# Grouped heads in two attention stages of a two-block transformer kernel on one core

## The reference, cut to what matters

```
def sliding_window_attention_with_sinks(q, k, v, sinks):   # 12 query heads, 4 key heads, 64 wide
    ...                                                    # each query block of 128 sees its own and the previous block
    scores = jnp.where(mask[None, :, None, None], scores, NEG_INF)
    m = jnp.maximum(jnp.max(scores, axis=-1, keepdims=True), sink)
    e = jnp.exp(scores - m)
    probs = e / (jnp.sum(e, axis=-1, keepdims=True) + jnp.exp(sink - m))
    out = jnp.einsum("bnkgqc,bnckd->bnqkgd", probs.astype(v.dtype), vb)

def memory_attention(q, mk, mv):                           # 4 heads, 64 wide, 256 memory tokens
    s = jnp.einsum("bshd,bmhd->bhsm", q, mk).astype(jnp.float32) * (HEAD_DIM ** -0.5)
    p = jax.nn.softmax(s, axis=-1).astype(mv.dtype)
    o = jnp.einsum("bhsm,bmhd->bshd", p, mv)
```

## Time and profile before

| what | value |
|---|---|
| median of 3 runs | 2321.39 us (2320.91 to 2326.01) |
| profiled execution, its own time | 2317.27 us |
| span of the profiled execution | 2315.3 us |
| TensorE busy | 2062.4 us, 89% |
| VectorE busy | 1187.1 us, 51% |
| ScalarE busy | 1000.4 us, 43% |
| mean granted TensorE clock | 0.914 |

### The profile page before, as it was taken

The page is one execution under the profiler, slowest core; times in us unless marked ns, Lnnn a source line. Parts: engine busy times, 40 slices in busy tenths (PEclk is TensorE's granted clock), DMA queues, the critical chain, the costliest instruction groups (busy, mean ns, idle before and its releaser), DMA issues.

```text
span 2315.3 us, 41908 instructions
## 1 busy us (share of the span) xinstructions
PE 2062.4 (89%) x16886; PEld 1777.1 (77%) x16886; DVE 1187.1 (51%) x1933; ACT 1000.4 (43%) x1636; POOL 139.1 (6%) x122
## 2 busy tenths in 40 slices
PE   5998999889999999998788899987789997788998
PEld 4883787777877877887778799976579986357997
DVE  5321787725433433545455376455466556546654
ACT  5332577324322323544322265447255554325543
POOL 0000000001000001002332000100010000001000
PEclk8999999869999999899999799999699999559999
DMA  8330576502333332322000166643246663004664
GB/s 264 86 114 9 154 222 188 164 8 78 105 91 91 100 91 85 98 78 81 4 3 3 33 174 185 193 118 100 73 128 189 176 180 109 0 1 139 186 174 119
DMA packets 441805, 254.62 MB, mean 110 GB/s; under 512 B 10816, under 2 KB 440512, under 8 KB 441536
## 3 DMA queue, kind: packets, MB, share of 16 engines
q1 hardware_dynamic: 441664, 252.59, 37.6%
HBM read 251.51 MB, written 1.05 MB: 109 GB/s over the span
## 4 chain that ended last, share of the span: by engine, by line
PE 81%; DVE 10%; ACT 6%; issue 2%; DMA 1%; POOL 0%; DVEq 0%; ACTq 0%; SPq 0%; POOLq 0%
PE bank L378 19%; PE bank L380 19%; PE bank L379 19%; PE bank L370 4%; PE bank L941 2%; PE bank L603 2%; PE bank L604 2%; DVE weights_lo L328 2%; PE bank L1876 2%; ACT weights_hi L321 1%; PE bank L947 1%; PE bank L1168 1%; PE bank L1978 1%; PE bank L611 1%; PE bank L1892 1%
## 5 line engine op out<-in xcount | busy, mean ns | idle before, releaser
L328 DVE TENSOR_TENSOR weights_lo<-ring,weights_hi 128x1024 fp32r<-128x1024 f32 x472 | 577.7, 1229 | 472.3 <-ACT weights_hi L321 468.9
L378 PE MATMUL bank<-x_hi,weights_hi 128*128 128x256 f32 (+1 forms) x2024 | 646.7, 320 | 80.9 <-DVE x_lo L406 29.0
L321 ACT ACTIVATE weights_hi<-ring 128x1024 fp32r<-128x1024 f32 x472 | 495.4, 1054 | 348.5 <-PE bank L380 311.6
L380 PE MATMUL bank<-x_hi,weights_lo 128*128 128x256 f32 (+1 forms) x2024 | 640.5, 316 | 0.0
L379 PE MATMUL bank<-x_lo,weights_hi 128*128 128x256 f32 (+1 forms) x2024 | 640.2, 316 | 0.0
L378 PEld LDWEIGHTS bank<-x_hi,weights_hi 128*128 128x128 f32 x2024 | 391.5, 193 | 115.2 <-issue 86.8
L379 PEld LDWEIGHTS bank<-x_lo,weights_hi 128*128 128x128 f32 x2024 | 391.7, 194 | 25.3 <-issue 1.2
L380 PEld LDWEIGHTS bank<-x_hi,weights_lo 128*128 128x128 f32 x2024 | 391.5, 193 | 23.4
L378 PE MATMUL bank<-hidden_hi,weights_hi 128*128 128x256 f32 (+1 forms) x864 | 271.0, 314 | 10.0 <-DVE hidden_lo L1442 6.8
L380 PE MATMUL bank<-hidden_hi,weights_lo 128*128 128x256 f32 (+1 forms) x864 | 269.7, 312 | 0.0
L379 PE MATMUL bank<-hidden_lo,weights_hi 128*128 128x256 f32 (+1 forms) x864 | 268.9, 311 | 0.0
(11 more groups left out here) (312 smaller groups left out, 2500.5 us busy)
## 6 DMA issues: line engine op xcount, KB each, us to landing
ring<-mlp_w SPq DMA_DIRECT2D x128, 512.0 KB, 4.0
ring<-ada_w SPq DMA_DIRECT2D x96, 512.0 KB, 4.7
ring<-w_ffn_in SPq DMA_DIRECT2D x88, 512.0 KB, 4.7
ring<-w_ffn_out SPq DMA_DIRECT2D x32, 512.0 KB, 3.8
ring<-gdn_w_in SPq DMA_DIRECT2D x24, 512.0 KB, 3.9
ring<-even_w_in SPq DMA_DIRECT2D x18, 512.0 KB, 4.7
ring<-w_out SPq DMA_DIRECT2D x16, 512.0 KB, 4.9
ring<-w_in_a SPq DMA_DIRECT2D x14, 512.0 KB, 3.8
```

What stands on the lines that cost most here:

```text
L321: nc.scalar.activation(w_hi[:, g % AHEAD, :], ring[:, g % RAW, :], ACT.Copy).then_inc(hi_done[g % AHEAD].sem, 1)
L328: nc.vector.tensor_tensor(w_lo[:, g % AHEAD, :], ring[:, g % RAW, :], w_hi[:, g % AHEAD, :].bitcast(F32), ALU.subtract).then_inc(lo_done[g ...
L378: pe.matmul(dst, lhs[0](k), rhs[0](k), start=start and k == 0, stop=False)
L380: last = pe.matmul(dst, lhs[1](k), rhs[0](k), start=False, stop=stop and k == nk - 1)
```

## The change

Both attentions are now run by a new class, `Grouped`, over groups of heads. In a memory attention a group is two heads and a block of 128 queries: 4 groups for each attention. In the sliding-window attention there are six groups of two heads for the second query block (256 keys) and four groups of three heads for the first (128 keys). The heads of a group are every second one, so that their outputs have the same half of the partitions and go out in one copy. For a group VectorE has one mask addition, one maximum, one negation, one reciprocal, one multiplication (by a reciprocal that is broadcast along each head's columns) and one copy of the output. ScalarE still has one exponential for each head, and one copy of the transposed probabilities for each group. TensorE has the same matmuls and transposes as before, in another order: scores of group i, transposes of group i-2, product of group i-3. Scores have three PSUM banks, probabilities three rooms.

A sink is a further column of its head's scores, written by GpSimd (scaled by 8, since the exponential scales by 1/8), so that the maximum and the sum take it in by themselves. VectorE waits for GpSimd's column ahead of the maximum.

In layer B the memory groups stand first; they need no rotated queries. The three rotations of the queries are done by VectorE after the maximum of groups 0, 1 and 2. The scores of the sliding-window groups wait for all five rotations, and no longer the first scores.

```
+            def pe(self, pe, ready=None):
+                for i in range(self.n + 3):
+                    if i < self.n:
+                        ...
+                        self.wait(pe, att_max, i - 3)
+                        self.wait(pe, att_exp, i - 3)
+                        for x, hd in enumerate(self.groups[i]["heads"]):
+                            ins = pe.matmul(self.scores(i)[:, x, :], hd["q"], hd["k"], start=True, stop=True)
+                        ins.then_inc(att_scores.sem, 1)
+                    if 0 <= i - 2 < self.n:
+                        j = i - 2
+                        g, (to, _) = self.groups[j], self.turned(j)[0]
+                        self.wait(pe, att_probs, j)
+                        self.wait(pe, att_probsT, j - 2)
+                        for x in range(len(g["heads"])):
+                            for b in range(g["nk"] // P):
+                                at = x * g["nk"] + b * P
+                                ins = pe.transpose(to[:, at:at + P], self.probs(j)[:, x, b * P:(b + 1) * P], ident)
+                        ins.then_inc(att_turned.sem, 1)
+                    if i - 3 >= 0:
+                        j = i - 3
+                        g, (_, pt) = self.groups[j], self.turned(j)[0]
+                        self.wait(pe, att_probsT, j)
+                        self.wait(pe, att_out, j - 2)
+                        for x, hd in enumerate(g["heads"]):
+                            ins = product(pe, self.mixed(j)[:, x * P:(x + 1) * P], lambda b: hd["v"][b],
+                                          lambda b: pt[:, x * g["nk"] + b * P:x * g["nk"] + (b + 1) * P], len(hd["v"]))
+                        ins.then_inc(att_mixed.sem, 1)
+
+            def dve(self, dve, between=None):
+                for i in range(self.n + 3):
+                    if i < self.n:
+                        g, src = self.groups[i], self.scores(i)
+                        self.wait(dve, att_scores, i)
+                        self.wait(dve, att_probs, i - 3)
+                        if "mask" in g:
+                            self.wait(dve, att_turned, i - 3)
+                            m = g["mask"].rearrange("p (o k) -> p o k", o=1).broadcast_to((P, len(g["heads"]), g["nk"]))
+                            link(dve, nc.vector.tensor_tensor(self.probs(i), src, m, ALU.add))
+                            dve.wait_ge(att_sinks.sem, self.sunk[i])
+                            src = self.wide(i)
+                        link(dve, nc.vector.reduce_max(self.small(i, 0), src, AX.X))
+                        nc.vector.tensor_scalar(self.small(i, 1), self.small(i, 0), -self.scale, None, ALU.mult)\
+                            .then_inc(att_max.sem, 1)
+                        if between is not None:
+                            between(dve, i)
+                    if 0 <= i - 1 < self.n:
+                        j = i - 1
+                        g = self.groups[j]
+                        self.wait(dve, att_exp, j)
+                        link(dve, nc.vector.reciprocal(self.small(j, 3), self.small(j, 2)))
+                        r = self.small(j, 3).rearrange("p (h o) -> p h o", o=1).broadcast_to((P, len(g["heads"]), g["nk"]))
+                        nc.vector.tensor_tensor(self.probs(j), self.probs(j), r, ALU.mult).then_inc(att_probs.sem, 1)
+                    if i - 3 >= 0:
+                        j = i - 3
+                        self.wait(dve, att_mixed, j)
+                        nc.vector.tensor_copy(self.groups[j]["out"], self.mixed(j).rearrange("p (h t) -> p h t", t=P))\
+                            .then_inc(att_out.sem, 1)
...
+            def pool(self, pool):
+                for i in self.sunk:
+                    self.wait(pool, att_turned, i - 3)
+                    nc.gpsimd.tensor_copy(self.wide(i)[:, :, self.groups[i]["nk"]], self.groups[i]["sinks"])\
+                        .then_inc(att_sinks.sem, 1)
...
+        att_b = Grouped(memory_groups(1) + swa_groups, HD ** -0.5)
...
-            att_b.pe(pe, lambda pe, i: pe.wait_ge(B["roped"].sem, 5) if i == 0 else None)
+            att_b.pe(pe, lambda pe, i: pe.wait_ge(B["roped"].sem, 5 if i >= 4 else 2))
...
-            nc.vector.tensor_scalar(nsink, sinks, -1.0, None, ALU.mult).then_inc(B["small"].sem, 1)
+            nc.vector.tensor_scalar(nsink, sinks, HD ** 0.5, None, ALU.mult).then_inc(B["small"].sem, 1)
...
-            dve_rotate(dve, qs, 3, 2)
-            att_b.dve(dve)
+            att_b.dve(dve, lambda dve, i: dve_rotate(dve, qs, i, 2) if i < 3 else None)
```

More of the change, by code:

```diff
@@ L2355, in two_block_kernel @@
         mq = ca(2, LAT)
-        att_room = [ca(T) for _ in range(4)] + [tmp[:, 0, :], tmp[:, 1, :]]
+        prob_room = [ca(T + 2) for _ in range(3)]
+        rot_room = [ca(T)] * 2
         qs = xc
@@ L2496, in two_block_kernel @@
                              [mv[:, l, i, :] for i in range(2)]) for l in range(2)]
-        def memory_units(l):
-            return [dict(q=mq[half(hd % 2), hd // 2, q:q + P], k=mk[half(hd % 2), l, hd // 2, :],
-                         v=[mv[:, l, b, hd * HD:(hd + 1) * HD] for b in range(2)], rows=half(hd % 2),
-                         out=mix[half(hd % 2), 6 + hd // 2, q:q + P]) for hd in range(MEMH) for q in (0, P)]
-        mem_att_a = Attention(memory_units(0), HD ** -0.5, att_room)
+        att_sinks = sig("att_sinks")
@@ new lines, in memory_groups @@
+        def memory_groups(l):
+            groups = []
+            for par in range(2):
+                for q in (0, P):
+                    heads = [dict(q=mq[half(par), hd // 2, q:q + P], k=mk[half(par), l, hd // 2, :],
+                                  v=[mv[:, l, b, hd * HD:(hd + 1) * HD] for b in range(2)]) for hd in range(par, MEMH, 2)]
+                    groups.append(dict(heads=heads, nk=NMEM, rows=half(par), out=mix[half(par), 6:8, q:q + P]))
+            return groups
+        mem_att_a = Grouped(memory_groups(0), HD ** -0.5)
@@ L2567, in two_block_kernel @@
         sinks = vector("sinks_2")
[L2568 to L2578 removed]
+        swa_groups = []
+        for qb, size in ((1, 2), (0, 3)):
+            nk = (qb + 1) * P
+            for first in range(0, SQH // 2, size):
+                for par in range(2):
+                    members = []
+                    for hd in range(2 * first + par, 2 * (first + size), 2):
+                        kv = hd // (SQH // SKH)
+                        kx = kv // 2 + (0 if kv % 2 == par else 2)
+                        members.append(dict(q=qs[half(par), hd // 2, qb * P:(qb + 1) * P], k=shk[half(par), kx, 0:nk],
+                                          v=[shv[:, b, kv * HD:(kv + 1) * HD] for b in range(qb + 1)]))
+                    swa_groups.append(dict(heads=members, nk=nk, rows=half(par), mask=window[:, 2 * P - nk:2 * P],
+                                           sinks=nsink[:, 2 * first + par:2 * (first + size):2],
+                                           out=mix[half(par), first:first + size, qb * P:(qb + 1) * P]))
+        att_b = Grouped(memory_groups(1) + swa_groups, HD ** -0.5)
         out_x.append(Operand(lambda k: mix[:, k, 0:LAT], KB, slice(0, LAT)))
@@ L2612, in pool_second @@
                 x.norm.pool_add(pool)
+                if x is ffn_a.post:
+                    pool.wait_ge(B["small"].sem, 4)
+                    att_b.pool(pool)
         def pe_second(pe):
@@ L2704, in act_second @@
             att_b.act(act)
-            act.wait_ge(att_out.sem, att_b.b[att_out.sem] + len(att_b.units))
+            act.wait_ge(att_out.sem, att_b.b[att_out.sem] + att_b.n)
             for k in range(KB):
```

89 lines of the change are left out of this document (64 added, 25 removed).

## The result

The changed kernel takes 2233.57 us (median of four runs, 2226.11 to 2245.06), beside 2321.15 for the kernel before: ratio 0.9627, 95% interval [0.958, 0.9674]. That is faster, as forecast, but 33 us under the forecast of 2267 and 6 under the low end of its range. Run again beside other kernels it took 2244.42 against 2319.66, ratio 0.968 [0.9649, 0.9711]. The profiled execution is the slowest of the first four: 2245.06 us, span 2243.3.

A forecast was written before the change was run, and what follows sets the result against it. TensorE, at 1.2 GHz and waiting in both second-block attentions, was taken as the bound. Gains of 9.3 (layer A), 40.3 (last attention) and 4.5 (clock) make 54 us: 2321.4 - 54 = 2267 us, range 2240 to 2280.

The forecast's parts named there:

- low end: Bottom of the whole kernel's forecast range: 2240 us, from the early clock rise's 2245 less 5.
- The step's price: TensorE's step of two 256-key heads at 1.2 GHz: scores 2.00, transposes 1.04, product 1.89, together 4.93 us.
- the clock's 3.0: Layer A's memory attention: clock rises over most of its last 6 us, 3.0 us gained.
- the rival: Last attention: clock rises early, VectorE sets steps of some 2.8 us, whole 2245 us; chance 0.36 including a halfway rise.
- bounds of 0 and 0.84: GpSimd's sink copies in ten masked groups: 0 taken; 0.84 us each uncovered, 8.4 us in all, put into the range.
- The failed step: Both attentions: clock rises only in last steps without scores; in the last attention no more than 0.5 us gained.
- the clock's 6.7: Clock gain of both attentions and the projections behind: 4.4 on layer A plus 2.3 on the last; two thirds, 4.5, counted.
- halfway rise: Last attention: clock rises partway through, whole 2256 us; chance 0.36 together with the early rise.
- 452 to 485: Earlier trace: 33 us of full TensorE, mostly 64-row matmuls, stayed at clock 0.50; used against an early rise.
- the doubt about transposes: Both attentions: transposes may not count as busy for the clock; then neither stage rises, 49.6 us gained, whole 2272 us.
- The other rivals: VectorE or GpSimd dearer, 2267 to 2280 us, 0.05; slower through sink waits, or groups not forming, 0.03 together.

The follow-up runs named there:

- e3: Changed kernel with each product directly behind its own group's transposes, a skew of two steps instead of three: 2283.2 us, ratio 0.983 to the kernel before.
- e2: Changed kernel with one head in each group, all else kept: 2284.2 us, ratio 0.981 to the kernel before.
- e5: Changed kernel with identity transposes (32 and 44) in TensorE's gap ahead of each stage's first transposes: 2234.5 us, ratio 0.963 to the kernel before.
- e1: Kernel before with two identity matmuls between transposes and product of each unit, in both attention stages: 2321.0 us, ratio 0.999.
- e10: As e3, with two identity matmuls between transposes and product of each group: 2257.2 us, ratio 0.971 to the kernel before.
- e7: Kernel before with identity matmuls only in the gaps ahead of both attention stages, none inside: 2315.1 us, ratio 0.997.
- e15: Kernel before with identity matmuls ahead of both stages and inside the last attention's first eight units: 2315.3 us, ratio 0.998.
- e6: Changed kernel with identity matmuls (16 and 22) in TensorE's gap ahead of each stage's first transposes: 2236.6 us, ratio 0.965 to the kernel before.
- e12: Changed kernel with identity matmuls in TensorE's gaps, product copies on ScalarE, q x cos on GpSimd: 2236.1 us, ratio 0.963 to the kernel before.

## Why the prediction was right and wrong

**Right, at 1.2 GHz.** The step's price was 2.00 + 1.04 + 1.89 = 4.93 us; layer A and e3 show 2.0 for scores, 1.04 to 1.11 for transposes and 1.90 for the product. The first transposes of the last attention were forecast 10.5 us behind the rotation matmuls (1970.25 less 1959.79) and came 10.6 behind (1962.96 less 1952.39). Layer A was forecast to end 17.7 us behind its first scores with the clock's 3.0; it ended at 1662.88, 17.6 behind. The projections behind the two stages gave 1.9 us each where 1.4 and 1.8 stood.

**Right, on the other engines.** VectorE's 2.9 us for a masked step were 2.67 to 2.90, 2.78 in the mean; it is the 2.8 that the rival used. GpSimd's copy of 2 columns took 0.19 us against bounds of 0 and 0.84, and VectorE waited for none.

**Wrong: the clock.** The failed step is to let the clock rise only where no scores are left, and so "in the last attention too late to give more than 0.5". It rose at 1969.9, with nine groups' scores still to come, 3.3 us into the first transposes and product that follow one another. The stage was forecast 70.8 us from rotations to last copy and took 48.7 (1952.39 to 2001.04): 22 us, two thirds of the miss. All of it lies behind the start of scores 4, which was forecast 17.1 us behind the rotation matmuls and came 17.2 behind; from there to the last copy 53.7 us were forecast, at 1.2 GHz, and 31.5 taken. Another 2.2 us are what I held back of the clock's 6.7; the remaining 9 no stage explains. I had the early rise as a rival and priced it nearly right: 50.2 us for the same stretch, 76 in all, where 78.7 were measured. I gave it, with a halfway rise, a chance of 0.36. What misled me was 452 to 485, mostly matmuls with 64 rows (24.9 of the 33 us), held against a step that is 59% transposes and products, which I called two thirds. In e2, whose steps hold the same 59% in shorter pieces, the clock did stay down as in that stretch; in groups it did not. One reading was also loose: in layer A's stretch something was loaded (37 GB/s in the earlier trace rows, where I wrote that nothing was), but nothing in the sum rests on it.

**Wrong: the doubt about transposes.** The rule I cited from the Trainium skill, TensorE: Matmul & The Clock Gate, section Part 4: PE-mode transpose, says that the full clock doesn't engage for transposes, since they don't count as busy in the same way. e5 disagrees: 5.03 us of transposes and nothing else held 1.00 (its row for 1952 to 1956), where the changed kernel's idle gap fell to 0.50. By this rule e5's layer A would have fallen; it took 15.3 us, as with matmuls. Here the measurement decides, for keeping the clock; whether transposes alone would also raise it no run shows. The doubt took 2.2 us off the forecast gain.

**Wrong: the width.** The low end, 2245 less 5, held the rival's time but no scatter of a run around it. The rival gave 2245. That the profiled run took just that is luck, for its untouched first stretch was 6.2 us longer than before's; the median of the four runs is 11 us lower, the repeated one 2244.4. Between the two medians of the same kernel lie 11 us, and the untouched first stretch alone moves by 20. The other rivals did not occur: no wait of VectorE for the sinks, and no step without its group.

**Still open** is why one head at a time (e2, e1) stays at 0.50 with TensorE busy 98%, whether e10 rose for the wait that went or for the matmuls that came, and what tips e7 and e15 apart in layer A.

## What to carry to other kernels

Price a stage once for each level of the granted clock and ask of each gap and each phase what it does to the level: with either of two parts missing the change gave 38 us, with both 75 to 88, for only with both was TensorE back at 2.4 GHz. Removing an engine's waits can be worth more than the waits, and a stop of 2 us between dense steps can cost two more steps at half speed. Where a median scatters by 10 us, compare the stages in the traces first.

## What the runs showed of the hardware

Transposes alone hold the clock: 5.03 us of them at 1.00 (e5). TensorE busy 98% to 99% of 70 to 95 us can stay at 0.50 (e1, e2). Filling a gap with otherwise useless 128x128 identity matmuls bought 3.4 us in layer A (e6) and, in the old order, 8.3 in one execution and 2.8 in another (e7, e15). Scores of 64 rows from different halves of the partitions ran at the same time: three groups took 2.10 us at 1.00 where one takes 1.06. Groups of one head from each half might use that; no run tries it. GpSimd multiplied 128x512 float32 by a broadcast row in 2.08, 1.09 and 1.09 us (4.18 for the three in e12), VectorE in 0.68. VectorE's operations of 512 columns beside it stayed at 0.69, but one negation took 0.84 instead of 0.17.
